# Stick-breaking with queries on partitions and a scan along the keys, in a two-layer hybrid attention trunk

## The reference, cut to what matters

```python
z = jnp.einsum('bthd,bshd->bhts', q, k).astype(jnp.float32) * SB_SCALE
before = k_pos[None, :] < q_pos[:, None]
log_keep = jnp.where(before, jax.nn.log_sigmoid(-z), 0.0)
later = lax.cumsum(log_keep, axis=3, reverse=True) - log_keep
a = jnp.where(before, jnp.exp(jax.nn.log_sigmoid(z) + later), 0.0)
return jnp.einsum('bhts,bshd->bthd', a.astype(v.dtype), v)
```

## Time and profile before

| what | value |
|---|---|
| time, median of 3 runs | 1141.88 us (1140.55 to 1141.94) |
| profiled execution, its own time | 1140.39 us |
| its span | 1138.5 us |
| TensorE busy, matmul | 1088.2 us, 96% |
| VectorE, ScalarE, POOL busy | 527.2, 445.1, 497.4 us |
| chain of waits, TensorE's share | 78% |
| TensorE's granted clock | 0.998 |

### The profile page before, as it was taken

How to read it: one execution, slowest core, us unless ns; L and a number is a source line. 1 busy time by engine, 2 the same in 40 slices (tenths; PEclk the granted TensorE clock), 3 DMA queues, 4 the chain that set the end, 5 groups by cost and what they waited for, 6 DMA issues and landing times.

```text
span 1138.5 us, 18633 instructions
## 1 busy us (share of the span) xinstructions
PE 1088.2 (96%) x7693; PEld 954.8 (84%) x7693; DVE 527.2 (46%) x1063; ACT 445.1 (39%) x770; POOL 497.4 (44%) x334
## 2 busy tenths in 40 slices
PE   2899999999999999999998999999999999999997
PEld 1878997768888999998788699777788899999975
DVE  7438996763442311001570799877433341001127
ACT  1344336564444532222223523465544462223220
POOL 3223345534443845354424145544334465444550
PEclk9999999999999999999999999999999999999999
DMA  6522343011111222523226123301111012242232
GB/s 199 195 75 76 112 154 115 3 37 38 37 38 37 75 75 77 200 76 111 85 99 185 50 85 106 122 6 39 38 37 39 18 58 92 95 166 75 78 107 83
DMA packets 70455, 96.67 MB, mean 85 GB/s; under 512 B 4586, under 2 KB 61252, under 8 KB 69732
## 3 DMA queue, kind: packets, MB, share of 16 engines
q1 hardware_dynamic: 66068, 82.74, 22.3%
q0 software_dynamic: 3872, 11.64, 3.1%
q10 hardware_dynamic: 432, 1.11, 0.4%
HBM read 79.53 MB, written 14.78 MB: 83 GB/s over the span
## 4 chain that ended last, share of the span: by engine, by line
PE 78%; DVE 11%; POOL 3%; ACT 3%; DMA 2%; issue 1%; SPq 0%; DVEq 0%; POOLq 0%; ACTq 0%
PE ps L499 35%; PE ps L828 9%; PE ps L802 8%; PE ps L693 5%; PE ps L757 4%; DVE attn L1243 3%; DVE top L1240 3%; PE ps L600 2%; PE ps L670 2%; PE ps L584 2%; PE ps L779 2%; PE ps L728 2%; PE ps L642 2%; PE ps L653 2%; DMA raw<-in_w_in 2%
## 5 line engine op out<-in xcount | busy, mean ns | idle before, releaser
L1394 POOL TENSOR_TENSOR w_lo<-raw,w_hi 128x1024 fp32r<-128x1024 f32 (+1 forms) x116 | 281.7, 2429 | 377.6 <-ACT w_hi L879 373.1
L499 PE MATMUL ps<-xT_hi,w_hi 128*128 128x288 f32 x992 | 294.2, 297 | 3.3 <-POOL w_lo L1394 3.3
L499 PE MATMUL ps<-xT_hi,w_lo 128*128 128x288 f32 x992 | 292.3, 295 | 0.0
L499 PE MATMUL ps<-xT_lo,w_hi 128*128 128x288 f32 x992 | 292.2, 295 | 0.0
L499 PEld LDWEIGHTS ps<-xT_hi,w_hi 128*128 128x128 f32 x992 | 186.1, 188 | 5.5 <-POOL w_lo L1394 4.3
L499 PEld LDWEIGHTS ps<-xT_lo,w_hi 128*128 128x128 f32 x992 | 186.1, 188 | 0.0
L499 PEld LDWEIGHTS ps<-xT_hi,w_lo 128*128 128x128 f32 x992 | 186.1, 188 | 0.0
L879 ACT ACTIVATE w_hi<-raw 128x1024 fp32r<-128x1024 f32 (+1 forms) x116 | 121.0, 1044 | 96.6 <-PE ps L499 70.8
L1355 DVE TENSOR_TENSOR qy<-qy,ps 128x576 f32<-128x576 f32 x32 | 24.1, 755 | 254.7 <-PE ps L499 254.7
L928 ACT ACTIVATE qy<-ps,bias 128x576 f32<-128x576 f32 x40 | 29.7, 743 | 159.1 <-PE ps L499 156.2
L499 PE MATMUL ps<-late_y_hi,w_hi 128*128 128x288 f32 x256 | 75.6, 296 | 0.0
(11 more groups left out here) (182 smaller groups left out, 2233.8 us busy)
## 6 DMA issues: line engine op xcount, KB each, us to landing
raw<-in_w_in SPq DMA_DIRECT2D x44, 1024.0 KB, 5.2
raw<-in_w_out SPq DMA_DIRECT2D x8, 1024.0 KB, 5.0
x_kept<-x_nat SPq DMA_DIRECT2D x2, 2560.0 KB, 11.4
x_nat<-x_kept SPq DMA_DIRECT2D x2, 2560.0 KB, 11.3
raw<-in_w_proj_a SPq DMA_DIRECT2D x8, 512.0 KB, 3.6
raw<-in_w_proj_b SPq DMA_DIRECT2D x8, 512.0 KB, 4.6
x_nat<-in_x_prompt SPq DMA_DIRECT2D x4, 512.0 KB, 9.0
out<-stage POOLq DMA_DIRECT2D x8, 256.0 KB, 4.1
```

The source lines that it names most:

```text
L499: last = mm(out, a, b[:, HALF * half:HALF * (half + 1)], start=(k == 0 and i == 0), stop=(k == n - 1 and i == 2))
L1394: g.tensor_tensor(lo, src, hi.bitcast(f32), ALU.subtract).then_inc(s_lo, 1)
```

## The change

Branch A now has queries on partitions and keys along the row. A chunk is prompt tile 3 for two heads (512 keys each), tiles 2 and 0 (384 and 128), or tile 1 (256) with the sample queries of both heads (320 keys): 1024, 1024 and 832 columns. VectorE adds the mask while it takes the scores from PSUM (mask_z), POOL clamps, ScalarE does exp and ln, VectorE takes the maximum and then runs a scan backwards along the keys, one instruction a row block (A_ROWS). POOL subtracts the sums from the scores (log_weight), ScalarE takes exp, TensorE transposes the weights (stick_transpose) three chunks later, ScalarE moves them out of PSUM (move_weights), and TensorE multiplies by the values. Scores have one slot in PSUM and three in SBUF. The stage holds 16 halves of dense units, uncut, so GA 3 moves into it. The first chunk is begun in the last softmax rounds. In the softmax rounds the QA matmuls stand in 22 groups of 2 to 4 k, behind the value products, and POOL builds the first two masks before its split of the first QA unit. The masks as bf16 rows are made once at the start, and ScalarE waits in layer 1 for layer 0's stores before it writes stage. Silu of GA 3 is now a step of its own.

The core of the diff (declarations and removed functions are left out; those stand in the kernel above):

```diff
-QA_GAP = 11
-QA_HALF_AT = {(QA_GAP * n + 7) // 4: n for n in range(8)}
+QA_GROUPS = [(n, ks) for n in range(8)
+             for ks in (((0, 1, 2, 3), (4, 5, 6, 7)) if n in (0, 7) else ((0, 1, 2), (3, 4, 5), (6, 7)))]
+QA_HALF_AT = {p: n for p, (n, ks) in enumerate(QA_GROUPS) if ks[-1] == 7}
...
-Z_SLOTS = 2
-E_SLOTS = 3
-A_UNITS = 7
+A_LAG = 3
+A_UNITS = 8
 Y_ORDER = [4, 5, 6, 7, 0, 1, 2, 3]
-SP_SLOTS = 4
-
-Z_BLOCKS = {0: [(2, 0, 256), (3, 256, 128)], 1: [(1, 0, 384)], 2: [(0, 0, 512)]}
-Z_SAMPLE = {0: [(1, 0), (2, 1)], 1: [(0, 0)], 2: []}
-S_COL = 384
-SP_AT = {j: (c, at) for c, blocks in Z_BLOCKS.items() for j, at, _ in blocks}
-SS_AT = {b: (c, hh) for c, blocks in Z_SAMPLE.items() for b, hh in blocks}
+
+A_TILES = ([(3, 0, 512)], [(2, 0, 384), (0, 384, 128)], [(1, 0, 256)])
+A_WIDTH = (1024, 1024, 832)
+A_ROWS = ([(0, 512), (512, 512)], [(0, 384), (384, 128), (512, 384), (896, 128)],
+          [(0, 256), (256, 256), (512, PAST + DEC)])
+A_MASK_AT = (0, 128, 256)
+S_HALF = (PAST + DEC) // 2
...
-        e_slot = [view(o_x, 2, 512), view(o_x + 1024, 2, 512), stage[:, :, 0:512]]
-        assert o_x + 2048 + 2 * SP_SLOTS * 1024 == REGION
+        z_at = (o_x + 7808, o_x, o_x + 2688)
+        z_slot = [view(at, 1024) for at in z_at]
+        sp_slot = [view(at, 1024) for at in (o_x + 8832, o_x + 1664, o_x + 3712)]
+        wt_slot = [view(at, 2, 512) for at in (o_x + 4736, o_x + 5760)]
...
+                def qa_group(n, ks):
...
+                    for k in ks:
+                        for i, (a, b) in enumerate(((hi, xT_hi), (hi, xT_lo), (lo, xT_hi))):
+                            last = mm(ps[:, 7, 0:HALF], a[:, k, :], b[:, k, cols],
+                                      start=(k == 0 and i == 0), stop=(k == 7 and i == 2))
+                    if ks[-1] == 7:
                         last.then_inc(s_grp if n % 2 else s_qh, 1)
...
                 def stick_z(p):
                     m, c = divmod(p, A_CHUNKS)
+                    if c == 0:
+                        pe.wait_ge(s_ev, L * (N_WO - 8) + act_evacs(N_QA + m) + 1)
+                    if p == 0:
+                        pe.wait_ge(s_rm, L * N_B + N_B - 2)
+                    else:
+                        pe.wait_ge(s_zm, L * NP + p)
+                    for i, at, nk in A_TILES[c]:
                         for hh in range(2):
                             half = slice(64 * hh, 64 * hh + 64)
+                            last = mm(ps[:, hh, at:at + nk], q_a[half, m, 128 * i:128 * i + 128],
+                                      kT_a[half, m, PAST + DEC:PAST + DEC + nk], start=True, stop=True)
+                    if c == 2:
+                        for n in range(2):
+                            last = mm(ps[:, n, 256:256 + S_HALF], q_s[:, m, :, :],
+                                      kT_a[:, m, S_HALF * n:S_HALF * n + S_HALF], start=True, stop=True)
                     last.then_inc(s_z, 1)
...
+                def stick_transpose(p):
+                    c = p % A_CHUNKS
+                    a = z_slot[p % 3]
+                    pe.wait_ge(s_aw, L * NP + p + 1)
+                    if p == 0:
+                        pe.wait_ge(s_rm, L * N_B + N_B)
+                    else:
+                        pe.wait_ge(s_wt, L * NP + p)
                     for hh in range(2):
+                        for i, at, nk in A_TILES[c]:
+                            for b in range(i + 1):
+                                src = (256 if c == 2 else 512) * hh + at + 128 * b
+                                bank, dst = (2, src) if c == 2 else (2 + hh, at + 128 * b)
+                                last = nc.tensor.transpose(ps[:, bank, dst:dst + 128], a[:, src:src + 128], ident)
+                    if c == 2:
+                        for b, kn in enumerate(SS_KEYS):
+                            last = nc.tensor.transpose(ps[0:kn, 3, 128 * b:128 * b + 128],
+                                                       a[:, 512 + 128 * b:512 + 128 * b + kn], ident)
+                    last.then_inc(s_at, 1)
...
+                    wt = wt_slot[p % 2]
+                    pe.wait_ge(s_wt, L * NP + p + 1)
+                    if p == 0:
+                        pe.wait_ge(s_yb, L * NBP + NBP)
+                        pe.wait_ge(s_ev, L * (N_WO - 8) + act_evacs(N_G))
+                    elif c == 0:
                         pe.wait_ge(s_ya, L * 2 * PAIRS + 2 * m)
...
+                pe.wait_ge(s_ev, L * (N_WO - 8) + act_evacs(N_QA))
+                for p in range(NBP + 3):
+                    if p < NBP:
+                        logits(p)
+                    if p == 2:
+                        pe.wait_ge(s_trev, L * N_TR + N_TR)
+                    if 2 <= p < NBP + 2:
+                        transpose_probs(2 * p - 4)
+                        transpose_probs(2 * p - 3)
+                    if p == NBP + 1:
+                        stick_z(0)
+                    if p >= 3:
+                        weigh_values(p - 3)
+                    if p < len(QA_GROUPS):
+                        qa_group(*QA_GROUPS[p])
+
+                for p in range(NP + A_LAG):
+                    if p >= A_LAG:
+                        stick_transpose(p - A_LAG)
+                    if 1 <= p < NP:
                         stick_z(p)
-                    dense_half(p, (0, 1, 2, 3, 4))
-                    if 1 <= p < NP + 1:
-                        stick_sum(p - 1)
-                    if p >= 2:
-                        stick_values(p - 2)
-                    dense_half(p, (5, 6, 7))
+                    dense_half(p, range(8))
+                    if p >= A_LAG:
+                        stick_values(p - A_LAG)
+                dense_half(NP + A_LAG, range(8))
...
+                def log_term(p):
+                    x = sp_slot[p % 3][:, 0:A_WIDTH[p % A_CHUNKS]]
+                    act.wait_ge(s_min, L * NP + p + 1)
+                    act_f(x, x, ACT.Exp).then_inc(s_e, 1)
+                    act.wait_ge(s_e, L * NP + p + 1)
+                    act_f(x, x, ACT.Ln, bias=one_eps[:, 0:1]).then_inc(s_ln, 1)
...
+                    if p == NBP + 1:
+                        log_term(0)
...
+                    x = z_slot[p % 3][:, 0:A_WIDTH[p % A_CHUNKS]]
+                    act_f(x, x, ACT.Exp).then_inc(s_aw, 1)
...
+                def move_weights(p):
+                    act.wait_ge(s_at, L * NP + p + 1)
+                    if p >= 2:
+                        act.wait_ge(s_av, L * NP + p - 1)
+                    wt = wt_slot[p % 2]
+                    if p % A_CHUNKS == 2:
+                        act_f(wt[0:DEC, 1, 256:384], ps[0:DEC, 3, 256:384], ACT.Copy)
+                        flat = wt.rearrange("p a n -> p (a n)")
+                        act_f(flat[:, 0:768], ps[:, 2:4, :].rearrange("p a n -> p (a n)")[:, 0:768],
+                              ACT.Copy).then_inc(s_wt, 1)
+                    else:
+                        act_f(wt, ps[:, 2:4, :], ACT.Copy).then_inc(s_wt, 1)
...
+                        elif L:
+                            act.wait_ge(s_ka_st[m % 2], L * 64)
...
+                for p in range(NP + A_LAG):
+                    if p >= A_LAG:
+                        move_weights(p - A_LAG)
+                    if 1 <= p < NP:
                         log_term(p)
                     if 1 <= p < NP + 1:
                         weights(p - 1)
                     if p % 2 == 1:
                         evacuate(N_G + p // 2)
                         head(N_G + p // 2 + 2)
+                evacuate(N_G + A_UNITS - 1)
+                head(N_G + A_UNITS + 1)
...
+                def mask_z(p):
+                    c = p % A_CHUNKS
+                    x = z_slot[p % 3]
+                    dve.wait_ge(s_z, L * NP + p + 1)
+                    if p >= 3:
+                        dve.wait_ge(s_at, L * NP + p - 2)
+                    else:
+                        dve.wait_ge(s_pt, L * N_B + N_B)
+                    n = 256 if c == 2 else 512
+                    if c == 2:
+                        v.tensor_tensor(x[:, 512:512 + 2 * S_HALF].rearrange("p (a k) -> p a k", a=2),
+                                        ps[:, 0:2, 256:256 + S_HALF],
+                                        before_s[:, :].rearrange("p (a k) -> p a k", a=2), ALU.add)
+                    v.tensor_tensor(x[:, 0:2 * n].rearrange("p (a k) -> p a k", a=2), ps[:, 0:2, 0:n],
+                                    for_both(before[:, A_MASK_AT[c]:A_MASK_AT[c] + n]), ALU.add).then_inc(s_zm, 1)
+                def softplus(p):
+                    w = A_WIDTH[p % A_CHUNKS]
+                    x = sp_slot[p % 3][:, 0:w]
+                    dve.wait_ge(s_ln, L * NP + p + 1)
+                    v.tensor_tensor(x, x, z_slot[p % 3][:, 0:w], ALU.max).then_inc(s_sp, 1)
+                    dve.wait_ge(s_sp, L * NP + p + 1)
+                    for at, n in A_ROWS[p % A_CHUNKS]:
+                        a = sp_slot[p % 3][:, at:at + n]
```

(56 more changed lines are left out.)

208 lines of the change are left out of this document (45 added, 163 removed).

## The result

The changed kernel takes 1209.14 us (median of 4 runs, 1208.08 to 1210.12) against 1141.53 for the kernel before on the same chip: ratio 1.0593 [1.0575, 1.0612], 5.9% slower. Slower was forecast, 1169 us of it, and the range ended at 1187.

The account below looks back on a forecast made before the run. TensorE bounds the old kernel; after the change VectorE's serial loop bounds the stage. Profiled 1140.4 + 32 (stage) - 8 (softmax rounds) + 3.6 (after the stage) = 1168, 1169.5 with the median's offset, given as 1169 us; range 1138 to 1187.

Parts of the forecast that it names:

- the clamp: POOL's clamp in the stick-breaking stage, priced like a one-input cast: 1.16 us for 1024 columns.
- Rival 4: Clamp costs as much as POOL's two-input work: 1.2 us more a chunk, 14 a layer, 1196 us; chance 0.08.
- The loop: Stage's serial path from mask add to mask add through VectorE, POOL and ScalarE: 7.97 to 8.95 us a chunk.
- Scan: VectorE's backward scans in the stage run at two-pass price, 2.08 ns a column: two of 512 take 2.44 us.
- Rival 1: Scans run in one pass, 1.0 us less a chunk; stage falls some 13 us, total 1142; chance 0.15.
- The port: POOL's work blocks VectorE's two-SBUF-input instructions in the stage; w_lo splits in the way cost 8.9 us a layer.
- Rival 2: POOL and VectorE hardly collide in the stage: 9 us less a layer, total 1150; chance 0.15.
- The added wait: In the stage, TensorE's stick_values waits for ya_out behind softplus: 4.6 us, again at p = 9, 9.3 in all.
- The tail: Stage after its last scan: ya_out, values, transposes and dense halves in turn, 16.3 us.
- Softmax rounds: Masks built before a split and grouped QA matmuls shorten these rounds by net 4 us a layer, 8 in all.
- After the stage: PR waits for the last late_y_lo behind four dense units: some 1.8 us a layer, 3.6 in all.
- Rival 3: Faster, TensorE stays the bound: needs single-pass scan and no collisions; 1135 us, or 1110 with early ya_out; chance 0.1.

Follow-up runs that it names:

- clamp_copy: Changed kernel with POOL's clamp made a plain copy and ScalarE's exponential taking an eighth of z: 1169.51 us, ratio 1.0238.
- no_split: Changed kernel without POOL's w_lo splits of the weights inside the stage, their signals kept: 1195.51 us, ratio 1.0475.
- ya_early: Changed kernel with VectorE issuing the head's output before the softplus of the same round instead of behind it: 1185.63 us, ratio 1.0386.
- ya_mid_lw_dve: Changed kernel with clamp and log_weight on VectorE; next mask add, then head's output, before softplus; ScalarE's evacuation before the weights' exponential: 1104.94 us, ratio 0.9671.
- mid_clamp_pool: Changed kernel, order only: VectorE's next mask add, then head's output, before softplus; ScalarE's evacuation before the weights' exponential; clamp on POOL: 1130.15 us, ratio 0.9888.
- ya_mid: Changed kernel with clamp on VectorE; next mask add, then head's output, before softplus; ScalarE's evacuation before the weights' exponential: 1120.07 us, ratio 0.98.
- pipe: Changed kernel with VectorE issuing the head's output, then the next chunk's mask add, before softplus; clamp on POOL: 1155.37 us, ratio 1.0121.

## Why the prediction was wrong in size

**The term that failed is the clamp.** The prediction took 1.16 us from POOL's casts, "the nearer kind", over the two-input row of 2.45. It measures 2.76, dearer than either: 1.6 us too little in each of 8 wide chunks a layer and 1.3 in each of 4 narrow ones (2.28 against 0.97), 18 us a layer and 36 in all. clamp_copy gives POOL about the price that was forecast (1.04 us) and takes 1169.5, close to the 1169 that were forecast. How close is in part luck: its stage took 130.7 us against 133.0, its rounds 4.6 us shorter and its tail 2.3 longer than the sum has them, and the changed kernel's gain in the softmax rounds was smaller than forecast. Rival 4 (chance 0.08) was the right mechanism; it stopped at the two-input price, and at 1196. The step that failed is the choice by likeness, one input being taken for what sets the price. The slope behind the 1.16 was weak as well. It came from two single casts, and over all casts of these sizes the kernel before shows no slope between 128 and 256 columns:

```profile
L1469 POOL CAST attn<-mask 128x256 f32<-128x256 bf16 x4 | 1.6, 403 | 0.0
...
L1469 POOL CAST attn<-mask 128x128 f32<-128x128 bf16 x4 | 1.6, 392 | 2.8 <-DVE row_min L1261 2.8
```

That a plain copy of 1024 columns then took 1.04 us was good fortune for the cast's price, and it says nothing of the minimum's.

**The loop** stood as described: mask to mask through POOL and ScalarE. Between the starts of the first and the last maximum of layer 0, 256.94 and 381.24, lie 11 rounds of 11.3 us. The parts, measured against forecast: up to the first maximum 3.9 us (1.8), the rounds with splits and waits 124.3 (93.0 + 8.9 + 9.3 = 111.2), last softplus 3.2 (3.7), tail 19.7 (16.3); in all 151.1 against 133.0. The first and second carry the clamp: 8 x 1.6 + 4 x 1.3 = 18 us, against 15.2 found, so the other terms there were some 3 us too dear, the scans above all (4 scans 2.44 us against 2.75, 3 scans 1.99 against 2.2).

**Scan.** Right, as said: 1.17 us for 512 columns against 1.22. By the Trainium skill, "DVE: opcode table, instruction layouts, handler registers and perf-mode slots", section "Datapath and trigger behaviour", the built-in scan runs at half throughput; the trace agrees, with 2.29 ns a column in the pair of 512, against 1.21 in the maximum over 1024 (1.24 us). Rival 1 falls.

**The port.** Right in kind and nearly in place. Three of layer 0's 12 sets of scans took 2.1 us more than alone, at chunks 0, 1 and 7 as forecast, and two splits held the clamps of chunks 4 and 6 for 1.0 us each (0.9 forecast). no_split gives 6.8 us a layer against 8.9. Rival 2 falls: splits do meet scans.

**The added wait.** Forecast 9.3 us in the rounds at p = 6 and 9; there the maxima stand 15.45 and 16.1 us apart, where the other rounds take 9.0 to 12.0. ya_early gives 11.8 us a layer. Some of what is above 9.3 is the clock: right after these waits the value products took 1.98 us where they take 1.02 in the tail (lines below), at a granted clock of 0.50.

**The tail.** Forecast 16.3 us at the full clock. The granted clock was 0.82 on the mean of the stage, that is, TensorE was at its 1.2 GHz level for parts of it. It was low behind stretches in which TensorE had stood waiting: 0.50 from 324.4 to 326.4, after 6.87 us of wait, and 0.54 from 383.43 to 389.27, after 5.71; from 391.32 on it was 1.00. Chain of waits, 16 value products twice and two dense halves of the same 24 matmuls:

```profile
324.43 1.98 PE ps L749 x16
...
383.43 5.84 PE ps L774 x24
389.27 1.02 PE ps L749 x16
...
391.32 3.20 PE ps L774 x24
```

The halves differ by 2.6 us, the tail's excess but for 0.8. With the products and transposes behind the two added waits (some 3.5 us) the low clock cost layer 0 an estimated 6 us on the chain. The prediction had no term for it.

**Softmax rounds.** 72.9 us against 75.5 before (180.60 to 256.15): 2.6 a layer, 4 forecast. The first masked logits waited 5.20 us for TensorE's scores in place of 7.83 for POOL.

**After the stage.** PR began at 432.2, right behind the last late_y_lo (429.31, 2.77 us), 28.1 us after the stage; four dense units are 25.4, so the wait is 2.7, forecast 1.8.

**Rival 3**, TensorE bound, is what ya_mid_lw_dve comes near, in another order and with two passes on another engine. The prediction took VectorE's order as given, which is right for a forecast of this diff, and did not price how much of the loop the order made.

**Two sums don't come out as printed.** TensorE's terms for a pair of heads add up to 21.1 us, 7.0 a chunk, not 20 and 6.8. Collisions at half or double of 8.9 us a layer give 1160 to 1187 us, not 1155 to 1183. Neither enters the 1169.

## What to carry to other kernels

When a new chain runs over four engines, write down for each engine what stands in its program between two links, and try to start item p+1 before finishing item p. Here the order alone was worth 79 us (1209.1 to 1130.2), and the dear instruction 39.6 us in the bad order but 10.1 in the good one (mid_clamp_pool to ya_mid). If taking away one wait gives nothing, look in the trace for the one right behind it before calling it harmless; here two waits in a row paid only together. An instruction whose operation no row shows is not priced safely by its number of inputs. It can even lie outside the bounds that other operations give (1.2 and 2.5 us here, 2.76 measured), and where it stands in a loop of 12 the forecast has to carry both bounds and say that neither was seen.

## What the runs showed of the hardware

- POOL over 1024 f32 columns: copy 1.04 us, subtraction of two inputs 2.35 to 2.40, minimum with a constant 2.76. The pass with one input and arithmetic is the dearest of the three. VectorE does that minimum in 0.69 us, a quarter.
- A clash at the port can lengthen both sides: the clamp on POOL goes from a median of 2.76 to 3.41 us in mid_clamp_pool, and VectorE's single scans reach 3.34 us against 1.17. In the clash at 258.20 the times fit instructions that take turns: the first scan ends at 259.34, the split, recorded from 258.33, at 261.59, or 2.25 us behind it, and the second scan at 262.67. So the 3.26 and 3.33 us would hold a wait each. This is a reading of starts and ends; no run tests it.
- The less TensorE waited in the stage, the higher its mean granted clock there: 0.82 in the change (busy 70%), 0.90 in pipe (81%), 0.97 in ya_mid (88%), 0.98 in ya_mid_lw_dve (93%). The higher clock is part of what the shorter waits gave back; how large a part was not separated.
